# Attention layer: the small matmuls of a pair of heads in three visits for scores and values instead of six, with other PSUM banks

## What is computed

```python
def dilated_attention_mixer(h, w_in, q_norm_w, k_norm_w, w_out):
    proj = h @ w_in                       # 3 groups x (q, k, v) x 16 heads x 64, and a gate
    for gi, (window, dilation) in enumerate(((128, 1), (512, 4), (2048, 16))):
        q, k = rms_norm(q_gi, q_norm_w[gi]), rms_norm(k_gi, k_norm_w[gi])
        scores = where(valid, q @ k.T / 8 - slope * distance, -1e30)
        lse = logsumexp(scores); p = exp(scores - lse); o_gi = p @ v
    weights = softmax(stack(lses))        # over the three groups, per head and token
    o = sum(weights[g] * o_g)
    return (o * silu(gate)) @ w_out
```

## Time and profile before

| | us |
|---|---|
| median of three runs | 1381.55 (1380.89 to 1382.06) |
| the profiled execution | 1381.57 |
| its span, first to last instruction | 1379.4 |
| TensorE busy (matmuls in flight) | 1370.8 |
| VectorE busy | 942.3 |
| ScalarE busy | 691.1 |
| GpSimd busy | 92.5 |
| DMA, mean over the span | 82 GB/s |

### The profile page before, as it was taken

One profiled execution on the slowest core, in us unless ns is written; L12 is line 12 of the kernel. 1 busy time (PEld: TensorE's weight loads), 2 busy tenths in 40 slices (PEclk: granted clock), 3 DMA queues, 4 the chain that ended last, 5 costly groups with the idle time before them and its releaser, 6 DMA issues.

```text
span 1379.4 us, 23267 instructions
## 1 busy us (share of the span) xinstructions
PE 1370.8 (99%) x9311; PEld 1147.6 (83%) x9311; DVE 942.3 (68%) x1666; ACT 691.1 (50%) x1211; POOL 92.5 (7%) x128
## 2 busy tenths in 40 slices
PE   9999999999999999999999999999999999999999
PEld 8888887898887878788878777799888988888878
DVE  7677778673667676667667676767657467777782
ACT  6444545353646465656565566464434344454450
POOL 2111212000000000000000000000000012111110
PEclk9999999999999999999999999999999999999999
DMA  6322233332222222222222221323333322232311
GB/s 189 93 77 77 62 88 98 99 93 76 77 77 77 77 77 77 77 76 77 77 77 77 67 62 56 98 73 92 95 89 92 107 78 76 62 92 77 88 52 61
DMA packets 211693, 113.69 MB, mean 82 GB/s; under 512 B 3744, under 2 KB 209890, under 8 KB 211587
## 3 DMA queue, kind: packets, MB, share of 16 engines
q1 hardware_dynamic: 211202, 112.02, 28.2%
q0 software_dynamic: 384, 0.20, 0.1%
HBM read 110.10 MB, written 2.10 MB: 81 GB/s over the span
## 4 chain that ended last, share of the span: by engine, by line
PE 94%; DVE 2%; ACT 2%; issue 1%; DMA 0%; SPq 0%; ACTq 0%; DVEq 0%
PE ps L594 38%; PE ps L609 37%; PE scores L609 4%; PE scores L977 2%; PE ps L1008 2%; PE ps L991 2%; PE scores L779 2%; PE ps L957 2%; PE ps L808 1%; PE ps L623 1%; PE ps L810 1%; PE scores L797 1%; PE scores L755 1%; DVE w_lo L1695 1%; PE ps L819 1%
## 5 line engine op out<-in xcount | busy, mean ns | idle before, releaser
L609 PE MATMUL ps<-w_hi,op_hi 128*128 128x512 f32 (+1 forms) x880 | 320.3, 364 | 3.5 <-DVE op_lo L1753 1.8
L594 PE MATMUL ps<-op_hi,w_hi 128*128 128x512 f32 (+1 forms) x800 | 317.8, 397 | 0.0
L609 PE MATMUL ps<-w_lo,op_hi 128*128 128x512 f32 (+1 forms) x880 | 309.5, 352 | 0.0
L609 PE MATMUL ps<-w_hi,op_lo 128*128 128x512 f32 (+1 forms) x880 | 308.8, 351 | 0.0
L594 PE MATMUL ps<-op_lo,w_hi 128*128 128x512 f32 (+1 forms) x800 | 305.5, 382 | 0.0
L594 PE MATMUL ps<-op_hi,w_lo 128*128 128x512 f32 (+1 forms) x800 | 304.9, 381 | 0.0
L1695 DVE TENSOR_TENSOR w_lo<-raw,w_hi 128x1024 fp32r<-128x1024 f32 x200 | 240.8, 1227 | 37.3 <-ACT w_hi L1198 36.7
L1198 ACT ACTIVATE w_hi<-raw 128x1024 fp32r<-128x1024 f32 x200 | 202.8, 1051 | 37.4 <-PE ps L609 13.0
L609 PEld LDWEIGHTS ps<-w_hi,op_hi 128*128 128x128 f32 x880 | 166.6, 189 | 29.1 <-issue 6.4
L609 PEld LDWEIGHTS ps<-w_lo,op_hi 128*128 128x128 f32 x880 | 166.4, 189 | 23.0
L609 PEld LDWEIGHTS ps<-w_hi,op_lo 128*128 128x128 f32 x880 | 166.9, 190 | 18.7 <-issue 0.2
(11 more groups left out here) (215 smaller groups left out, 1813.2 us busy)
## 6 DMA issues: line engine op xcount, KB each, us to landing
raw<-in_b_w_in SPq DMA_DIRECT2D x80, 512.0 KB, 3.9
raw<-in_a_w_in SPq DMA_DIRECT2D x64, 512.0 KB, 4.2
raw<-in_c_w_in SPq DMA_DIRECT2D x24, 512.0 KB, 4.8
raw<-in_a_w_out SPq DMA_DIRECT2D x16, 512.0 KB, 4.1
raw<-in_b_w_out SPq DMA_DIRECT2D x8, 512.0 KB, 4.0
raw<-in_c_w_out SPq DMA_DIRECT2D x8, 512.0 KB, 4.6
xt<-in_x SPq DMA_DIRECT2D x4, 512.0 KB, 6.2
y<-in_norm_w SPq DMA_DIRECT2D x3, 512.0 KB, 4.3
```

What stands on the lines that cost most here:

```text
L594: last = nc.tensor.matmul(bank, a, b, start=(k == 0 and p == 0), stop=(k == KT - 1 and p == 2))
L609: last = nc.tensor.matmul(bank, a, b, start=(k == 0 and p == 0), stop=(k == KT - 1 and p == 2))
```

## The change

The keys of the attention work get tables of their own. scores(0) and scores(1) run together at step 4; scores(2), scores(3), values(0), values(1) together at step 28; values(2), values(3) at step 53. The turns of p stand alone at 15, 25, 39 and 49. As two slots' scores now live at once, `slot_banks` puts those of slot 1 into `obank` and `spare` and those of slot 3 into the `turn` banks, and p of slots 1 and 3 goes to `b_qk[:, 0:2]`, the place of the undilated q and k. New or moved waits follow from that: scores(1) for the previous pair's `mg_sub` and `t_copied`, scores(3) for both copies of p(1), turn_p(2) for all four biases, values(0) for two biases, the first two `qk_out` for the previous pair's last values. In the eighth pair, whose order is written out, scores(1) moves to the front, values(1) up beside scores(3), values(2) down beside values(3); the lists of VectorE and ScalarE for it stay as they are. Sorted by the new keys, VectorE has unit(3) 32.5, split_lo 7 33.0, split_lo 8 33.1, bias(3) 33.5, peak(3) 33.6, normalise(2) 36.1, p_out(2) 39.9; ScalarE has unit(3) 32, chunks 7 and 8 at 32.1 and 32.2, exps(2) 32.5, exps(3) 38.5, p_out(2) 39.8.

```diff
--- before.py
+++ after.py
@@ -65,7 +65,12 @@
 B_TURNS = 7
 QK_TURNS = (0, 1, 2, 3, 5, 6, 7)
 B_SLOTS = 4
-SLOT_AT = (4, 15, 26, 38, 50, 62)
+SCORES_AT = (4, 28)
+BIAS_AT = (4.5, 14.5, 28.5, 33.5)
+EXPS_AT = (8.5, 18.5, 32.5, 38.5)
+NORMAL_AT = (10.4, 22.1, 36.1, 44.1)
+TURN_AT = (15, 25, 39, 49)
+VALUES_AT = (28, 53)
 
 
 LAYER_IN = (HEADS * A_CHUNKS, HEADS * B_CHUNKS, C_V_CHUNKS + C_UG_CHUNKS, HEADS * A_CHUNKS)
@@ -216,6 +221,7 @@
         b_s1, at = carve(at, 2, 2, 256)
         b_s = (b_s0, b_s1)
         b_pt, at = carve(at, 2, S)
+        b_p = (b_pt, b_qk[:, 0:2], b_pt, b_qk[:, 0:2])
         b_raw, at = carve(at, 3 * TT, 256)
         b_v, at = carve(at, 2, 2 * TT, P)
         b_vf, at = carve(at, S)
@@ -258,6 +264,7 @@
         turn = ps[4:6]
         obank = ps[6]
         spare = ps[7]
+        slot_banks = (score, (obank, spare), score, turn)
 
 
         s_ident = sem("s_ident")
@@ -961,8 +968,16 @@
                         stream = w // 2
                         if w % 2 == 0:
                             pe.wait_ge(qkT_done, h * B_TURNS + (6 if stream else 2))
-                        if w or later:
-                            pe.wait_ge(s_biased, h * B_SLOTS + w)
+                        if w == 0 and later:
+                            pe.wait_ge(s_biased, h * B_SLOTS - 1)
+                        if w == 1 and later:
+                            pe.wait_ge(mg_sub, h)
+                            pe.wait_ge(t_copied, h)
+                        if w == 2:
+                            pe.wait_ge(s_biased, h * B_SLOTS + 1)
+                        if w == 3:
+                            pe.wait_ge(pT_act, h * B_SLOTS + 2)
+                            pe.wait_ge(pT_dve, h * B_SLOTS + 2)
                         for k in range(2):
                             u = 2 * w + k
                             t = u % TT
@@ -974,13 +989,15 @@
                                         to, keys = slice((g - 1) * P, g * P), tile
                                     else:
                                         to, keys = slice(keys_from(u), 2 * P), slice(max(t - 1, 0) * P, (t + 1) * P)
-                                    last = nc.tensor.matmul(slot_half(score[e], k)[:, to], b_qk[head, 2 * g, tile],
+                                    last = nc.tensor.matmul(slot_half(slot_banks[w][e], k)[:, to], b_qk[head, 2 * g, tile],
                                                             b_qk[head, 2 * g + 1, keys], start=True, stop=True)
                                     if k == 1 and g != 1:
                                         last.then_inc(s_ready, 1)
 
                     def turn_p(w):
                         pe.wait_ge(p_done, h * B_SLOTS + (w + 1))
+                        if w == 2:
+                            pe.wait_ge(s_biased, h * B_SLOTS + B_SLOTS)
                         for e in range(2):
                             if w == 0:
                                 pe.wait_ge(qkT_done, h * B_TURNS + B_TURNS)
@@ -995,9 +1012,8 @@
                         stream = w // 2
                         pe.wait_ge(pT_act, h * B_SLOTS + (w + 1))
                         pe.wait_ge(pT_dve, h * B_SLOTS + (w + 1))
-                        if w % 2 == 0 and later:
-                            pe.wait_ge((mg_sub, t_copied)[stream], h)
                         if w == 0:
+                            pe.wait_ge(s_biased, h * B_SLOTS + 2)
                             pe.wait_ge(qkT_done, h * B_TURNS + B_TURNS)
                         for at in range(keys_from(w), 4 * P, P):
                             k, c = divmod(at // P, 2)
@@ -1006,7 +1022,7 @@
                             for e in range(2):
                                 head = slice(e * 64, e * 64 + 64)
                                 last = nc.tensor.matmul((obank, spare)[stream][head, t * P:(t + 1) * P], v[:, head],
-                                                        b_pt[:, e, at:at + P], start=(c == 0 or at == keys_from(w)),
+                                                        b_p[w][:, e, at:at + P], start=(c == 0 or at == keys_from(w)),
                                                         stop=(c == 1))
                         last.then_inc(bo_ready, 1)
 
@@ -1045,11 +1061,11 @@
 
                     if mix and not proj:
                         scores(0)
+                        scores(1)
                         turn_qk(2)
                         turn_qk(3)
                         first_half(0)
                         turn_qk(4)
-                        scores(1)
                         turn_qk(5)
                         first_half(1, 2)
                         turn_qk(6)
@@ -1060,16 +1076,16 @@
                         turn_p(1)
                         values(0)
                         scores(3)
+                        values(1)
                         first_half(5)
-                        values(1)
                         turn_p(2)
                         second_half(0)
-                        values(2)
                         first_half(6)
                         second_half(1)
                         turn_p(3)
                         second_half(2, 3)
                         turn_lse()
+                        values(2)
                         values(3)
                         second_half(4, 5, 6)
                         return
@@ -1078,14 +1094,11 @@
                     if mix:
                         for b in range(B_TURNS):
                             steps.setdefault(QK_TURNS[b], []).append(lambda b=b: turn_qk(b))
-                        for s in range(B_SLOTS + 2):
-                            at = steps.setdefault(SLOT_AT[s], [])
-                            if s < B_SLOTS:
-                                at.append(lambda w=s: scores(w))
-                            if s >= 2:
-                                at.append(lambda w=s - 2: values(w))
-                            if 1 <= s <= B_SLOTS:
-                                at.append(lambda w=s - 1: turn_p(w))
+                        for w in range(B_SLOTS):
+                            steps.setdefault(SCORES_AT[w // 2], []).append(lambda w=w: scores(w))
+                        for w in range(B_SLOTS):
+                            steps.setdefault(VALUES_AT[w // 2], []).append(lambda w=w: values(w))
+                            steps.setdefault(TURN_AT[w], []).append(lambda w=w: turn_p(w))
                         steps[57] = [turn_lse]
                     if static(i) and i == HEADS - 1:
                         steps[74] = [lambda: turn_qk(0, i, True)]
@@ -1429,6 +1442,8 @@
                         act.wait_ge(qkT_ready, h * B_TURNS + (b + 1))
                         if later:
                             act.wait_ge(s_ready, h * 8)
+                            if b < 2:
+                                act.wait_ge(bo_ready, h * B_SLOTS)
                         g, part = divmod(b, 2)
                         col = 18 + 3 * part + g
                         of, to = turn[b % 2][:], b_qk[:, b]
@@ -1458,10 +1473,10 @@
 
                     def p_out(w):
                         act.wait_ge(pT_ready, h * 8 + (2 * w + 1))
-                        if w or later:
-                            act.wait_ge(bo_ready, h * B_SLOTS + w)
+                        if w > 1 or w == 0 and later:
+                            act.wait_ge(bo_ready, h * B_SLOTS + w - 1)
                         first = keys_from(w)
-                        nc.scalar.activation(b_pt[:, 0, first:], turn[0][:, first:], ACT.Copy).then_inc(pT_act, 1)
+                        nc.scalar.activation(b_p[w][:, 0, first:], turn[0][:, first:], ACT.Copy).then_inc(pT_act, 1)
 
                     def log_sums():
                         act.wait_ge(e_done, h * 16 + 16)
@@ -1597,8 +1612,8 @@
                         for b in range(B_TURNS):
                             plan.append((QK_TURNS[b] + 1, v_out if b == 6 else lambda b=b: qk_out(b)))
                         for w in range(B_SLOTS):
-                            plan.append((SLOT_AT[w] + 4.5, lambda w=w: exps(w, (0, 1))))
-                            plan.append((SLOT_AT[w + 1] + 0.8, lambda w=w: p_out(w)))
+                            plan.append((EXPS_AT[w], lambda w=w: exps(w, (0, 1))))
+                            plan.append((TURN_AT[w] + 0.8, lambda w=w: p_out(w)))
                         plan.append((46, log_sums))
                         plan.append((58, weight_copy))
                         plan.append((63, dilated_out))
@@ -2142,7 +2157,7 @@
                                 to = slice((g - 1) * P, g * P) if stream else slice(0, 2 * P)
                                 dist = b_dist[:, 2 * P * stream:][:, to]
                                 ratio = slope[:, bass.ds(h * 2 + (16 * g + e), 1)]
-                                of = score[e][:].rearrange("p (k c) -> p k c", k=2)
+                                of = slot_banks[w][e][:].rearrange("p (k c) -> p k c", k=2)
                                 if w == 0:
```

(14 more changed lines are left out.)

## The result

| | us |
|---|---|
| median of four runs | 1416.31 (1416.14 to 1417.07) |
| before, on the same chip | 1381.61 (1380.89 to 1382.06) |
| ratio | 1.0253, 95% interval 1.0235 to 1.0270 |
| span of the profiled execution | 1414.4 (before 1379.4) |
| mean granted clock of TensorE | 0.989 (before 1.000) |

The account below looks back on a forecast made before the run. TensorE's instruction list was taken to bound the kernel. Per full pair -1.2 + 0.8 + 3.2 = +2.8 us, seven pairs +19.6, ends +1.0 and +0.5: +21.1 on 1381.57, stated as 1402.5 us, range 1395 to 1412.

Parts of the forecast that it names:

- What bounds the kernel: TensorE's instruction list, in flight 1370.8 of 1379.4 us; any wait of TensorE costs its full length.
- The price of a change, 0.18 us, and 1.2 us a pair: TensorE's attention visits: grouping cuts changes of array shape from 14 to 7 a pair, saving 1.2 us (1.05 to 1.4).
- turn_p(0), 0.1 us of margin: Turn of p(0) at step 15: normalise(0) is ready 0.1 us before TensorE arrives, so no cost.
- turn_p(1), 0.8 us: Turn of p(1) at step 25: TensorE waits 0.8 us (0.4 to 1.2) for normalise(1), perhaps partly at step 24.
- turn_p(2), 3.2 us: Turn of p(2) at step 39: TensorE waits 3.2 us (2.8 to 3.5) for normalise(2), now behind bias(3) and peak(3).
- Seven pairs and the turn_p(3) of the seventh: Full pairs: +2.8 us each, +19.6 together (14 to 25.5); +1.0 (0.5 to 1.5) at the seventh's turn_p(3).
- Pair eight, +0.5 us: Last pair: 0.9 us saved, scores(3) about 2 us late behind VectorE's p(1) copy, partly given back; +0.5 (-1 to +1.5).
- The clock: Rival, 8%: after each of seven 3.2 us idle stretches TensorE runs as long at 1.2 GHz; 11.2 us more, 1413.7 us.
- The faster side, 5%: Rival, 5%: waits at steps 32 to 39 hidden, about 1378 us, or changes of shape worth far more than 0.18 us.
- the case without either wait: Full pairs with no wait at turn_p(1) or turn_p(2): 1381.6 - 8.4 - 0.9 = 1372 us.

Follow-up runs that it names:

- the mended kernel: Changed kernel with bias and peak of slots 1 and 3 and exps(2) re-keyed, turn_p(2), turn_p(3) one step later, pair eight's p(1) copy earlier: 1371.98 us, ratio 0.9932.

## Why the prediction was right and wrong, point by point

**What bounds the kernel.** Right. With the clock held, the removed changes of shape and the new waits of TensorE showed up in the total at about their full length.

**The price of a change, 0.18 us, and 1.2 us a pair.** Right: 1.22 us measured in the mended kernel, 0.18 to 0.20 where two changes were put back. The visits at steps 28 and 53 of the changed kernel cost 3.87 and 2.10 us (forecast 3.9 and 2.1); this is the one at 28:

```profile
526.24 0.40 PE L616 MATMUL ps<-w_lo,op_hi 128*128 128x512 f32 x1
526.57 1.16 PE L992 MATMUL scores<-scratch 64*128 64x128 f32 x16
...
528.55 1.75 PE L1024 MATMUL ps<-scratch 128*64 128x128 f32 x28
...
530.57 0.39 PE L616 MATMUL ps<-w_hi,op_lo 128*128 128x512 f32 x1
```

**turn_p(0), 0.1 us of margin.** Right; it never waited.

**turn_p(1), 0.8 us.** Right: 0.86 us, with the part at step 24. From turn_p(0) to turn_p(1) TensorE takes 8.34 us in the changed kernel and 7.48 in the mended one, where nothing waits in between. (The idle times that the profile shows, about 0.2 us at each of the two places, are shorter than the loss, since matmuls overlap; the 0.65 us in two of the expectations was read too low from them.)

**turn_p(2), 3.2 us.** Right: 3.2 us (turn_p(2) 8.60 us after step 32, forecast 8.62). That the wait came from bias(3) and peak(3) in front of normalise(2) is shown by the kernel in which they were moved.

**Seven pairs and the turn_p(3) of the seventh.** With the clock held (idle time filled), these seven pairs took 520.2 us against 498.9 before: +21.2, forecast 19.6 + 1.0 = 20.6.

**Pair eight, +0.5 us.** Mis-sized: +1.5 us in the changed kernel (scores(0) to the residual's first matmul: 39.62 against 38.14), at the upper bound. The wait at scores(3), 2.2 us, was forecast as about 2; what I expected later waits to give back, they gave back only in part.

**The clock. This is the step that failed.** I had the mechanism as a rival, at 8% and 1413.7 us. The argument against it was that no idle time in the trace of before had lowered the clock, while the longest of those was 1.2 us. That says nothing on 3.2 us, and I let it weigh as if it did. The measured price in the seven pairs is 12.3 us net (forecast 11.2 under the rival): 1.4 to 2.9 us in each of the first six, and 0.2 in the seventh, where a TensorE slowed by the clock no longer meets the 1.3 us wait at turn_p(3). With it the sum is 1381.6 + 21.2 + 12.3 + 1.5 = 1416.6, and 1416.3 was measured. The rule of the Trainium skill ("TensorE: Matmul & The Clock Gate", Why this matters for your kernels) was named as speaking for the fall; the traces agree with it at the idle times of 3.0 and 3.25 us (14 of 14). They show falls already at 2.7 us (7 of 7) and in some executions at 2.2, which is under the gap that the section warns of. The range ended at 1412 because I cut off the larger part of a case that a forecast wait of 3.2 us, seven times, made the likely one.

**The faster side, 5%.** The mended kernel shows that it was there to be had, but only with other keys: 1372.0 us, where the case without either wait was put at 1372.

## What to carry to other kernels

A regrouping on the busiest engine is worth what its own trace says (here 0.18 us for each change of array shape), but it must be paid for in the lists of the other engines: put every new key in its place and compare, for each wait, the time at which the data are ready with the time at which the engine now arrives. If the sum contains idle times of TensorE of more than about 2 us (in these kernels 1.75 us was safe and 2.2 us was not), look at what the lower clock behind them would cost: here each 3.2 us wait cost 5.0 us on average (3.2 + 12.3 / 7). And a rival whose condition your own forecast fulfils is not a rival but a term of the sum.

## What the runs showed of the hardware

- In the profiled executions the granted clock fell to 0.50 at idle times of TensorE of 2.7, 3.0 and 3.25 us each time (21 of 21 at turn_p(2)), at 3 of 5 of those of 2.2 us (pair eight), and not at those of 1.75 us (0 of 7). It set in around the *end* of the idle time, between 1.25 us before it and 1.0 us after it (in the changed kernel 0.9 before to 0.8 after), so that nearly all of the lower clock fell on work.
- How long it lasted went with that moment. In the 18 falls that set in after the end of the idle time, or at most 0.69 us before it, it lasted 3.4 us; in the 7 that set in 0.71 us or more before it, twice as long.
- At 0.50 a 512-wide matmul follows the other at 0.427 us instead of 0.227, so a microsecond at the lower clock loses 0.47 us of work. The period of a pair was 74.1 us with the clock held and the same waits, 75.8 us with a short fall (iteration 3) and 77.0 us with one of twice the length (iteration 2).
- Thirteen matmuls whose result is thrown away, put into the idle time of each full pair, made the changed kernel 11.5 us faster (still 23.6 us slower than before, since the waits stayed).
